# The 64x64 inverses of a chunked RWKV-7 mixer: products on four quarters of TensorE, fewer levels, one PSUM bank for each direction

## The reference

```
def step(state, inp):
    r_t, w_t, k_t, v_t, a_t, b_t = inp
    sa = jnp.einsum('bhvk,bhk->bhv', state, a_t)
    state = (state * w_t[:, :, None, :] + sa[..., None] * b_t[:, :, None, :]
             + v_t[..., None] * k_t[:, :, None, :])
    return state, jnp.einsum('bhvk,bhk->bhv', state, r_t)
```

## Time and profile before

| | us |
|---|---|
| median of three runs | 2022.66 |
| lowest, highest | 2022.49, 2026.82 |
| the profiled execution | 2029.15 |
| its span in the profile | 2027.2 |
| TensorE busy in it | 1910.2 (94%) |
| VectorE busy | 1095.8 (54%) |
| ScalarE busy | 739.1 (36%) |

### The profile page before, as it was taken

One profiled execution on the slowest core, in us unless ns is written; L12 is line 12 of the kernel. 1 busy time (PEld: TensorE's weight loads), 2 busy tenths in 40 slices (PEclk: granted clock), 3 DMA queues, 4 the chain that ended last, 5 costly groups with the idle time before them and its releaser, 6 DMA issues. The chain is left out here.

```text
span 2027.2 us, 38671 instructions
## 1 busy us (share of the span) xinstructions
PE 1910.2 (94%) x16360; PEld 1748.5 (86%) x16360; DVE 1095.8 (54%) x1845; ACT 739.1 (36%) x1108; POOL 33.2 (2%) x62
## 2 busy tenths in 40 slices
PE   5999999998888989999999999999978898999997
PEld 2888999995665879999999999999747497999997
DVE  3544444865537466554455554476564756655533
ACT  3333333435224244333343333344441424433322
POOL 0000000000001000000000000000000100000000
PEclk9999999998789999999999999999979798999999
DMA  7766233423446233333343333442240401333332
GB/s 271 263 224 222 90 129 137 158 101 113 142 129 212 85 109 125 124 124 113 127 145 124 124 118 114 138 169 90 87 148 4 159 13 66 125 124 124 105 128 89
DMA packets 73192, 263.25 MB, mean 130 GB/s; under 512 B 9696, under 2 KB 10848, under 8 KB 56928
## 3 DMA queue, kind: packets, MB, share of 16 engines
q1 hardware_dynamic: 73056, 261.27, 37.9%
HBM read 259.08 MB, written 2.16 MB: 129 GB/s over the span
## 5 line engine op out<-in xcount | busy, mean ns | idle before, releaser
L157 PE MATMUL ps<-h_head,w_head 128*128 128x386 f32 x1824 | 624.0, 342 | 9.2 <-DVEq L243 4.1
L157 PE MATMUL ps<-h_head,w_rest 128*128 128x386 f32 x1824 | 619.3, 340 | 0.0
L157 PE MATMUL ps<-h_rest,w_head 128*128 128x386 f32 x1824 | 617.3, 338 | 0.0
L219 ACT ACTIVATE w_head<-w_raw 128x2048 fp32r<-128x2048 f32 (+1 forms) x176 | 303.0, 1721 | 609.2 <-PE ps L157 598.9
L222 DVE TENSOR_TENSOR w_rest<-w_raw,w_head 128x2048 fp32r<-128x2048 f32 (+1 forms) x176 | 360.7, 2049 | 204.4 <-ACT w_head L219 204.3
L157 PEld LDWEIGHTS ps<-h_head,w_head 128*128 128x128 f32 x1824 | 345.9, 190 | 28.6 <-issue 18.8
L157 PEld LDWEIGHTS ps<-h_head,w_rest 128*128 128x128 f32 x1824 | 345.8, 190 | 0.0
L157 PEld LDWEIGHTS ps<-h_rest,w_head 128*128 128x128 f32 x1824 | 343.0, 188 | 0.2
L157 PE MATMUL ps<-gu_head,w_head 128*128 128x384 f32 x832 | 279.9, 336 | 11.4 <-DVE gu_rest L813 11.4
L157 PE MATMUL ps<-gu_rest,w_head 128*128 128x384 f32 x832 | 279.4, 336 | 0.0
L157 PE MATMUL ps<-gu_head,w_rest 128*128 128x384 f32 x832 | 279.3, 336 | 0.0
(11 more groups left out here) (294 smaller groups left out, 1798.1 us busy)
## 6 DMA issues: line engine op xcount, KB each, us to landing
w_raw<-in_w_in SPq DMA_DIRECT2D x88, 1024.0 KB, 4.8
w_raw<-in_w_out SPq DMA_DIRECT2D x64, 704.0 KB, 4.0
w_raw<-in_ada_w SPq DMA_DIRECT2D x41, 1024.0 KB, 6.2
ada_raw<-in_ada_w SPq DMA_DIRECT2D x31, 1024.0 KB, 6.4
w_raw<-in_mix_in SPq DMA_DIRECT2D x26, 1024.0 KB, 4.9
w_raw<-in_mix_out SPq DMA_DIRECT2D x8, 1024.0 KB, 5.0
hyena_const<-in_hconst SPq DMA_DIRECT2D x2, 1792.0 KB, 9.6
x<-in_x_in SPq DMA_DIRECT2D x1, 1536.0 KB, 12.2
```

The costliest lines, as they stand in the source:

```text
L157: return nc.tensor.matmul(out, lhsT, rhs, start=start, stop=stop)
L219: return nc.scalar.activation(self.HI[src], self.RAW[src], ACT.Copy)
```

## The change

- The steps of one pair's inverse are done for both z at once. `crossed` gives z = 0 to the diagonal quarters and a bank, z = 1 to the other two quarters (rows of head h, columns of head 1-h) and the next bank. A result of z = 1 then lies on the other half of the partitions; the next crossed product brings it back. `straight` does both z on the diagonal, one after the other.
- The factors are others: with J2 = I + X2, J4 = I + X4, J8 = I + X8 the product T = (I + D), J2 T, J4 T, J8 T is the inverse of the blocks; then EX and G = its transpose, JE = I + EX, y1 = JE Q, EX2 = G EX, JG = I + EX2, and Y = JG y1. Products: before 264 of 64 columns and 24 of 128 for a pair, after 336 of 64.
- Copies of both banks at once (768 columns) by ScalarE or VectorE; I + ... is an addition on VectorE. Copies of x4 and ex are made beside the additions.
- A pair has four neighbouring banks (0 to 3, 4 to 7 for the other) instead of a shared bank 6; bank 7 is that of the conditioning too, so pair B's first square waits for the first set's bias and the second set waits for B's y1 to be copied.
- `pool_q` makes I + D instead of I + X.
- The lists are rewritten. In `two_pairs_stage` the second conditioning set moves from the gram products and the inverse into the recurrence, and pair A is a step ahead of B there. In `gla_and_pair_stage` its units 4 to 7 go ahead of `pe_x(0)`, and so do GLA's `norm` and, ahead of `pe_u(0)`, `spread`.

```diff
+            def crossed(self, ba, bb, lhsT, rhs):
+                for c in range(NCH):
+                    for h in range(2):
+                        mm(bank(ba, TOK)[half(h), c * C:c * C + C], lhsT[half(h), 0, c, :], rhs[half(h), 0, c, :])
+                    for h in range(2):
+                        last = mm(bank(bb, TOK)[half(1 - h), c * C:c * C + C], lhsT[half(h), 1, c, :], rhs[half(h), 1, c, :])
+                return last
+            def pe_d4(self, pe):
+                self.after_act(pe, "d2_1")
+                self.after_dve(pe, "x2_1")
+                self.pe_step(self.crossed(*self.even(), self.X, self.D2), "d4")
+            def pe_t1(self, pe):
+                self.after_dve(pe, "j2_1")
+                self.after_pool(pe, "q1")
+                self.pe_step(self.crossed(*self.odd(), self.J2, self.T), "t1")
+            def pe_x4(self, pe):
+                self.after_act(pe, "d4")
+                self.pe_step(self.crossed(*self.even(), self.D2, self.X), "x4")
+            def pe_t2(self, pe):
+                self.after_dve(pe, "j4")
+                self.after_act(pe, "t1")
+            def pe_x8(self, pe):
+                self.after_dve(pe, "x4")
+            def pe_t(self, pe):
+                self.after_dve(pe, "j8")
+                self.pe_step(self.straight(*self.odd(), self.J8, self.T), "t")
+            def pe_g(self, pe):
+                self.after_act(pe, "q")
+            def pe_y1(self, pe):
+                self.after_act(pe, "q")
+                self.after_dve(pe, "ex")
+            def pe_ex2(self, pe):
+                self.after_act(pe, "gm")
+                self.after_dve(pe, "ex")
+            def pe_y(self, pe):
+                self.after_dve(pe, "jg")
+                self.after_act(pe, "y1")
+                self.pe_step(self.straight(*self.even(), self.JG, self.Y1), "y")
...
+            def dve_one_plus(self, dve, product, out, banks, name):
+                self.after_pe(dve, product)
+                ones = cst("istack").unsqueeze(1).unsqueeze(1).to_broadcast([128, 2, NCH, C])
+                self.tt(out, self.both(banks), ones, ALU.add, name)
...
-                A = Pair(scope, SEMS[0:5], lay, 1, (0, 1, 2), 6, PR, TG, AL, MO)
-                B = Pair(scope, SEMS[5:10], lay, 2, (3, 4, 5), 6, PR, TG, AL, MO, (A.act_done, A.AC["s6_1"]))
+                A = Pair(scope, SEMS[0:5], lay, 1, (0, 1, 2), 3, PR, TG, AL, MO)
+                B = Pair(scope, SEMS[5:10], lay, 2, (4, 5, 6), 7, PR, TG, AL, MO, (SEMS[16], 1))
...
+                    ada_products(pe, 1, 0)
                     B.pe_u(pe, 0)
+                    ada_products(pe, 1, 1)
```

More of the change, by code:

```diff
@@ new lines, in straight, with even, odd @@
+            def straight(self, ba, bb, lhsT, rhs):
+                for z, b in enumerate((ba, bb)):
+                    for c in range(NCH):
+                        for h in range(2):
+                            last = mm(bank(b, TOK)[half(h), c * C:c * C + C], lhsT[half(h), z, c, :], rhs[half(h), z, c, :])
+                return last
+            def even(self):
+                return (self.b0, self.b1) if self.b3 > self.b2 else (self.b1, self.b2)
+            def odd(self):
+                return (self.b2, self.b3) if self.b3 > self.b2 else (self.b3, self.b0)
@@ L1513, in pe_s1 @@
                     pe.wait_ge(*self.shared_free)
[L1514 to L1530, removed]
@@ new lines, in pe_s1 @@
+                for b, lhsT, rhs in ((ba, self.X, self.D), (bb, self.D, self.X)):
+                    for c in range(NCH):
+                        for h in range(2):
+                            last = mm(bank(b, TOK)[half(h), c * C:c * C + C], lhsT[half(h), z, c, :], rhs[half(h), z, c, :])
+                self.pe_step(last, f"s1_{z}")
+            def pe_d4(self, pe):
+                self.after_act(pe, "d2_1")
+                self.after_dve(pe, "x2_1")
+                self.pe_step(self.crossed(*self.even(), self.X, self.D2), "d4")
@@ new lines, in pe_x8, with pe_q @@
+            def pe_x8(self, pe):
+                self.after_dve(pe, "x4")
+                self.pe_step(self.crossed(*self.even(), self.D4, self.X4), "x8")
+            def pe_t(self, pe):
+                self.after_dve(pe, "j8")
+                self.pe_step(self.straight(*self.odd(), self.J8, self.T), "t")
+            def pe_q(self, pe):
+                self.after_act(pe, "t_0")
+                self.after_dve(pe, "t_1")
+                for c in range(NCH):
+                    for h in range(2):
+                        mm(bank(self.even()[0], TOK)[half(h), c * C:c * C + C], self.INV[half(h), 0, c, :], cst("istack", 0, None, 64 * h, 64 * h + 64))
+                    for h in range(2):
+                        last = mm(bank(self.even()[1], TOK)[half(1 - h), c * C:c * C + C], self.INV[half(h), 1, c, :],
+                                  cst("istack", 0, None, 64 * h, 64 * h + 64))
+                self.pe_step(last, "q")
@@ L2224, in gla_and_pair_stage @@
             with ExitStack() as scope, nc.Block() as block:
[L2225 to L2226 removed]
+                A = Pair(scope, SEMS[0:5], lay, 0, (0, 1, 2), 3, PR, TG, AL, MO)
+                G = Gla(scope, SEMS[5:10], lay, (4, 5, 6), P, MO)
                 ADA = Ada(scope, SEMS[10:15], 2, [7] * sets, 1)
@@ L2605, in _ @@
+                    B.pe_y1(pe)
+                    B.pe_ex2(pe)
                     A.pe_state(pe, 0)
                     A.pe_out(pe, 0)
+                    B.pe_y(pe)
+                    A.pe_x(pe, 1)
+                    B.pe_x(pe, 0)
+                    A.pe_u(pe, 1)
+                    ada_products(pe, 1, 0)
                     B.pe_u(pe, 0)
-                    A.pe_x(pe, 1)
+                    ada_products(pe, 1, 1)
+                    A.pe_state(pe, 1)
+                    A.pe_out(pe, 1)
```

497 lines of the change are left out of this document (229 added, 268 removed).

## The result

| | before | after |
|---|---|---|
| median, us | 2024.88 (6 runs) | 2038.52 (6 runs) |
| lowest, highest | 2022.49, 2027.36 | 2031.67, 2044.64 |
| ratio to before | | 1.0069 [1.0052, 1.0086] |
| span of the profiled execution | 2027.2 | 2038.6 |

The account below looks back on a forecast made before the run. TensorE's stream was taken to bound the inverse phases, dependences the recurrences. Stage terms -5.4 - 3.0 - 3.8 - 2.6 = -14.8 us, from the median 2022.66 to 2007.9 us (-0.73%); range 1998 to 2020.

Parts of the forecast that it names:

- What bounds the kernel: Four inverse phases: TensorE's own stream sets the pace, busy 31.3 of 31.3 us in one; in the recurrences dependences decide.
- Price of a crossed step: Inverse steps of 24 products over four quarters: 0.70 us taken, bounds 0.70 and 1.40.
- Rival (a): Crossed steps: the quarters do not run four at a time, a step costs 1.40 us, total 2039; chance 0.10.
- Rival (b): Crossed steps: matmuls start at least 25 ns apart, a step costs 1.20 us, total 2030; chance 0.03.
- TensorE's sum: Inverse of each pair: 12.6 us of TensorE work, 5.5 less than before; 33 us less over six pairs.
- Layout and waits: Four mixer stages laid out engine by engine with copies and waits: -5.4, -3.0, -3.8 and -2.6 us.
- TensorE's waits on VectorE: Inverse phases: TensorE idle about 3 us a stage, released by VectorE.
- The wait for a conditioning load in layer 0: Layer 0, pairs 1 and 2: conditioning loads start three units earlier than their use, up to 2.5 us of wait.
- Recurrence and tail: Layer 1, pairs 1 and 2, behind `pe_x(0)`: pair 2's remaining work and `mean` give back some 3 us.
- Rival (e): Inverse phases: TensorE with gaps gets the half clock, one stretch up to 10 us, 2018; 0.07 with other no-change ways.
- What would show it: Trace signs: crossed steps 0.70 us apart, VectorE idle about 3 us a stage, `pe_x(0)` 11 to 12 us earlier.

Follow-up runs that it names:

- diagonal_after: Kernel after, with z = 1 of each crossed step also on the diagonal quarters (two quarters, same instructions): 2044.91 us, 1.0078 of before.
- wide_after: Kernel after, with crossed steps in half the instructions, products 128 columns wide, inverse not computed rightly: 2009.93 us, 0.9894 of before.
- repeat_d4: Kernel after, with the crossed step d4 of each mixer stage's first pair issued 16 times over: 2102.91 us in one run.
- added_loads: Kernel after, with seven added 1 MB loads by SyncE in layer 1's stage of pairs 1 and 2: 2050.72 us in one run.

## Why the prediction was wrong

*What bounds the kernel.* Right as far as it went: TensorE's stream set the pace of the inverse phases. I read it as its busy time and not as its number of instructions.

*Price of a crossed step.* Right, in short bursts: 0.70 to 0.75 us from start to start. Rival (a), steps of 1.40, is false, though its time of 2039 is what came out; an agreement in the total says nothing on the mechanism. Rival (b), 1.20, is false as well.

*TensorE's sum*, "ten steps 7.0 us. Sum 12.6 us a pair, 5.5 less than before". **This is the step that failed.** A pair's 336 products are 1344 instructions, at 3.48 to 3.75 us for 256 of them 18.3 to 19.7 us; before, 288 products are 1152 instructions in 18.1 us. The forecast of 12.6 us asked for 107 instructions a us. The row for `pe_between` that gave me the price (96 MATMUL and as many LDWEIGHTS records in 1.43 us) is shorter than one block, and a burst says nothing on what is sustained. The phase of layer 1 was to hold 1089 MATMUL and 1090 LDWEIGHTS records in 26.6 us, 82 a us; at 68 to 74 they need 29.4 to 32.0, and took 31.5. No row of before shows an inverse phase above that rate: the one of layer 1 has 1113 and 1114 in 38.25 us, 58 a us. The small products' own pace of 69 a us (48 instructions in 0.70 us) was already close to the limit, so over many such steps in a row four quarters had at most some 7% to give (74 against 69). In the whole phase of layer 1, which has waits and wider products too, they gave 3.9 of 35.4 us (`diagonal_after`). The -5.4 us forecast for this stage became +2.4: 4.9 of these 7.8 us were lost up to `pe_x(0)`, and the rest behind it.

*Layout and waits.* With the supply relieved, the layout came true: `pe_x(0)` 26.4 us behind the first square (forecast 26.6), in layer 0 with GLA 30.0 (29.9), and the four stages -3.4, -3.7, -3.5, -4.3 for the forecast -2.6, -3.0, -3.8, -5.4, of which 2.7 us in all come from the cheaper wide steps. The layout that rival (a) gives for steps of 1.40 is what `diagonal_after` runs, and it came out as well: +4.5, +6.5, +2.7 and +5.8 for the forecast +5, +6.5, +1.5 and +3.4, 3 us worse in the sum. So new factors and new order without the four quarters cost 19.5 us in the stages; the whole gain hung on the price of the crossed steps. TensorE's waits on VectorE were over-sized: 0.7 us and not 3, in `wide_after` too. The wait for a conditioning load in layer 0, put at up to 2.5 us, is 0.2.

*Recurrence and tail.* In layer 1 `pe_x(0)` to the end of pair 2's last product was to take 30.4 us and took 32.6; 1.1 us of it are stops.

*Rival (e), the half clock.* It came in layer 0 with GLA, for 6.8 us from within the stop of 3.97 us and for 3.4 us near the end of the phase, and in layer 1 with GLA for 3.4 us behind a stop of 1.12 us. With half of the instructions none of the three is there, so they go with the stops and not with the waits that I had in mind. I had given all such cases 0.07 together.

*What would show it.* "Wrong would be [...] a stage that ends later although its inverse is earlier": both pair stages do so. What I lacked was a rival in which TensorE is ready, its operands are ready, and its next instruction is not there.

## What to carry to other kernels

Count instructions beside columns: for a stretch of small products, records of MATMUL and LDWEIGHTS divided by the time you forecast must stay under the rate that the trace sustains from block to block (here 64 to 74 a us over several blocks of 256; the first blocks of a dense stretch can be faster, since their instructions lie ready), or the stretch is as long as its instructions need. Where it doesn't, idle quarters give little, and what helped here was a form with fewer and wider instructions. Idle time of TensorE with the releaser "issue" in the middle of a uniform step, 256 records from the last such gap, is the mark; in the two runs that changed the loads beside it, lighter ones shortened the gap and added ones lengthened it.

## What the runs showed of the hardware

- TensorE's instructions arrive in blocks of 256 records, in a dense stretch with no loads beside it 3.46 to 4.01 us apart (`repeat_d4`), and single blocks cost stops of 3.70 to 4.28 us while loads of 1 MB are under way. In the pair stage with its seven added loads six stops were over 1.3 us.
- An instruction packet of 16 KB takes 0.9 to 1.5 us, with loads beside it or without. Without loads it starts 1.0 to 1.7 us behind the first product of a block in the dense stretches of `repeat_d4`, with loads of 1 MB 2.9 to 5.0 us (`added_loads`, the kernel after at 550.76), most often as the load under way runs out.
- Products on four quarters issue at 24 in 0.70 us in bursts; on the two diagonal quarters a product takes 58 ns with 32 and with 64 columns, and 109 with 128 (0.655 us for six).
- In each of the four stops of 3.70 to 4.28 us the granted clock fell to 1.2 GHz, for 6.8 to 10.2 us. Shorter stops went both ways: in the pairs of layer 1 those of 1.4 to 2.33 us left it at 1.00 (`repeat_d4`, `added_loads`), in layer 0 with GLA it fell among stops of 1.2 to 1.92 us (`repeat_d4`).
- What happens before a packet starts, and between its end and the first product of the next block, can't be seen in the trace; so why blocks come 3.5 us apart, when a packet takes about 1, stays open.
